# The carry-over product of a windowed-mean pool in a MoE transformer layer: from 128 rows by 64 columns to 32 rows by 16 columns

## The reference, cut to what matters

```python
POOL_WINDOWS = (2, 4, 8, 16)
def multiscale_pool(u, pool_w, pool_scale):        # u: (1, 2048, 512)
    csum0 = jnp.pad(jnp.cumsum(uf, axis=1), ((0, 0), (1, 0), (0, 0)))
    for gi, w in enumerate(POOL_WINDOWS):          # 128 channels for each window
        upper = csum0[:, 1:, lo:hi]
        lower = csum0[:, jnp.maximum(t + 1 - w, 0), lo:hi]
        cnt = jnp.minimum(t + 1, w)
        outs.append((upper - lower) / cnt - uf[:, :, lo:hi])
    ...
h = modulate(rmsnorm(x, norm1_g), shift1, scale1);  proj = h @ w_in      # q, k, v, u
x = x + gate1 * (concatenate([attention(q, k, v), pool(u)]) @ w_out)
x = x + gate2 * moe_ffn(modulate(rmsnorm(x, norm2_g), shift2, scale2))
return rmsnorm(x, final_g)
```

## Time and profile before

| | |
|---|---|
| runs | 2816.91, 2818.95 and 2823.79 us, median 2818.95 |
| profiled execution | 2818.95 us, of which the span is 2817.0 us |
| granted TensorE clock, mean | 0.978 |
| PE busy | 2655.8 us, 94% of the span |
| DVE busy | 1435.9 us, 51% |
| ACT, POOL busy | 839.1 us, 807.4 us |
| chain that ended last | PE 73%, DVE 13%, DMA 8% |

### The profile page before, as it was taken

One profiled execution on the slowest core, in us unless ns is written; L12 is line 12 of the kernel. 1 busy time (PEld: TensorE's weight loads), 2 busy tenths in 40 slices (PEclk: granted clock), 3 DMA queues, 4 the chain that ended last, 5 costly groups with the idle time before them and its releaser, 6 DMA issues.

```text
span 2817.0 us, 46309 instructions
## 1 busy us (share of the span) xinstructions
PE 2655.8 (94%) x13342; PEld 1258.9 (45%) x13343; DVE 1435.9 (51%) x2391; ACT 839.1 (30%) x1304; POOL 807.4 (29%) x460
## 2 busy tenths in 40 slices
PE   4899999998899999999999999999999999999980
PEld 1477887786444333333333333333333333333330
DVE  4578888886433444444444444444444344444345
ACT  3344444443101222222222222222222222222224
POOL 0012222222211333333333233333333333333230
PEclk8999999999999999999999999999999999999995
DMA  8621121214536665888998987989889867869948
GB/s 346 227 76 66 69 75 67 75 67 143 199 111 225 209 212 171 299 286 303 344 337 296 341 299 255 340 291 336 296 297 325 311 180 256 302 212 344 369 115 357
DMA packets 140218, 664.09 MB, mean 236 GB/s; under 512 B 30276, under 2 KB 31173, under 8 KB 87575
## 3 DMA queue, kind: packets, MB, share of 16 engines
q1 hardware_dynamic: 89958, 528.96, 47.4%
q0 software_dynamic: 50224, 134.69, 21.6%
HBM read 569.55 MB, written 127.02 MB: 247 GB/s over the span
## 4 chain that ended last, share of the span: by engine, by line
PE 73%; DVE 13%; DMA 8%; issue 4%; ACT 1%; SPq 1%; DVEq 0%; ACTq 0%; POOLq 0%
PE PB L1497 35%; PE PB L1504 18%; PE PB L1339 5%; DMA arena<-in_w_up_e 5%; PE PB L1250 3%; PE PB L1274 2%; DMA arena<-in_ada_w 1%; PE PB L1510 1%; PE PB L1432 1%; DMA arena<-acc_tab 1%; PE PB L1396 1%; PE PB L1397 1%; PE PB L1401 1%; DVE arena L959 1%; PE PB L1418 1%
## 5 line engine op out<-in xcount | busy, mean ns | idle before, releaser
L1497 PE MATMUL PB<-arena 128*64 x2528 | 1111.5, 592 | 1.1 <-DVE arena L1132 1.1
L1498 PE MATMUL PB<-arena 128*64 128x512 f32 x2528 | 1111.5, 592 | 0.0
L606 POOL DMA_INDIRECT acc_tab<-arena,rec x157 | 480.3, 3059 | 1162.2 <-DVE rec L1168 785.5
L1497 PEld LDWEIGHTS PB<-arena 128*64 128x64 f32 x2528 | 346.5, 137 | 724.6 <-issue 724.6
L1504 PE MATMUL PB<-arena 128*64 x1264 | 606.3, 602 | 2.7 <-ACT arena L751 2.7
L1505 PE MATMUL PB<-arena 128*64 128x512 f32 x1264 | 606.3, 602 | 0.0
L1129 DVE COPY arena<-arena 128x4096 f32 x160 | 367.0, 2294 | 132.1 <-DMA arena<-in_w_up_e 61.1
L1165 DVE SCALAR_TENSOR_TENSOR arena<-PB,RW,arena 128x512 f32<-128x512 f32 x314 | 221.3, 746 | 273.2 <-PE PB L1505 215.9
L1498 PEld LDWEIGHTS PB<-arena 128*64 128x64 f32 x2528 | 346.6, 137 | 0.0
L564 POOL DMA_INDIRECT rec_tab<-recs,posi x128 | 144.2, 1126 | 626.7 <-DVE recs L953 589.9
L1135 DVE TENSOR_TENSOR arena<-arena,PB 128x256 f32<-128x256 f32 x158 | 96.3, 609 | 403.6 <-ACT arena L742 403.6
(11 more groups left out here) (277 smaller groups left out, 2629.8 us busy)
## 6 DMA issues: line engine op xcount, KB each, us to landing
arena<-in_w_gate_e SPq DMA_DIRECT2D x128, 1024.0 KB
arena<-in_w_up_e SPq DMA_DIRECT2D x128, 1024.0 KB, 10.4
arena<-in_w_down_e SPq DMA_DIRECT2D x128, 1024.0 KB, 10.3
arena<-in_ada_w SPq DMA_DIRECT2D x24, 1024.0 KB, 9.3
arena<-in_x SPq DMA_DIRECT2D x32, 512.0 KB, 3.4
acc_tab<-arena SPq DMA_DIRECT2D x32, 512.0 KB, 2.7
arena<-acc_tab SPq DMA_DIRECT2D x6, 2048.0 KB, 22.3
h_tab<-arena SPq DMA_DIRECT2D x16, 512.0 KB, 2.7
```

The source lines that it names most:

```text
L606: g.indirect_dma_start(acc_tab, bass.IndirectOffsetOnAxis(ap=rec[:, n, 1:2], axis=0), ys[n % 2], None, bounds_check=2 * T - 1, oob_is_err= ...
L1497: mm(B[7][0:SUB, :], xTm[:, k, 0:SUB], wa(k), start=(k == 0), stop=(k == KD - 1))
L1498: last = mm(B[7][SUB:P, :], xTm[:, k, SUB:P], WBG[n % 2][:, k], start=(k == 0), stop=(k == KD - 1))
```

## The change

The second product of each channel group uses 32 tokens of `uP` (partitions 96 to 127) in place of 128, and gives 16 output columns in place of 64. The band constant for it gets 16 columns for each group in place of 64, and ACT copies 32 partitions of `uC` to `uP` in place of 128.

```diff
 EDGE = 16
-NEAR = 64
-COLS = dict(ident=P, band0=NPG * EDGE, band=NPG * P, bandp=NPG * NEAR, iota=P,
+COLS = dict(ident=P, band0=NPG * EDGE, band=NPG * P, bandp=NPG * EDGE, iota=P,
             sub=4, half=1, inv=ROT, iotag=NG, tok=NT)
...
-        prev.append(((t - (s - P) < w) / w)[:, 0:NEAR])
+        prev.append(((t - (s - P) < w) / w)[:, 0:EDGE])
...
-                        ch.link(A_(uP, uC, ACT.Copy))
+                        ch.link(A_(uP[96:P, :], uC[96:P, :], ACT.Copy))
...
-                            last = mm(B[7][:, g_ * P:g_ * P + NEAR], uP[:, cs], C("bandp")[:, g_ * NEAR:(g_ + 1) * NEAR], start=False, stop=True)
+                            last = mm(B[7][:, edge], uP[96:P, cs], C("bandp")[96:P, es], start=False, stop=True)
```

## The result

The changed kernel takes 2836.69 us (median of 4 runs, 2831.63 to 2838.24), the kernel before beside it 2819.62 us (2816.91 to 2823.79). The ratio is 1.0055, with a 95% interval of 1.004 to 1.0072: slower by 0.55%, some 16 us. The forecast was slower, 2829.2 us, with a range of 2818 to 2838. The profiled execution took 2837.07 us, its span 2835.0. Two executions in the rounds of the experiments were far off, one of e6_rows64 (5379.73 us) and one of the kernel before (15735.44 us); ratios leave them out.

A forecast was written before the change was run, and what follows sets the result against it. PE was taken to bound the kernel, near balance with DVE. 14 tiles x 1.2 us less 6.5 us spare gave 10.3 us, so 2818.95 + 10.3 = 2829.2 us, range 2818 to 2838.

The forecast's parts named there:

- Columns, load rows, copy, constants: 0 each: Pool's carry product, its weight loads, ACT's copy and the start's constant load: making each smaller was taken to save 0.
- A change of shape, 0.20 in and 0.12 back, 1.2 us a tile: PE's pool: switching between 128-row and 32-row products drains PE, 8 times a tile, 0.32 us a group, 1.2 us a tile.
- Rivals A (under 0.07 us each): Pool: shape changes are cheap and the wait for DVE hides them, 2819 to 2820 us; chance 0.19.
- B (0.28 us each): Pool: shape changes are dear, 0.28 us each, 2.2 us a tile, giving 2843 us; chance of its side 0.08.
- C (a gain): Pool: 32-row loads cost a quarter and nothing drains, at most 1.3 us gained, 2817.6 us; chance 0.04.
- 0.54 us of it hidden in the wait for DVE: Attention-weight transposes behind the pool: PE already waits there for DVE in 12 tiles, hiding 0.54 us, leaving 0.66 us a step.
- the swallowing that was foreseen: DVE's L977 moves by up to 1.0 us, absorbed by 2.13 us of DVE idle time ahead of L999.
- In tile 15 the added time is hidden: Tile 15: PE idles 3.89 us for DVE ahead of L1339, independent of the pool, so its 1.2 us are hidden.
- the likeliest case: Pool's shape changes drain and cost between 0.13 and 0.2 us each, 2827 to 2834 us; chance 0.52.
- a sign for being wrong: The step growing by more than the pool would mean ACT's later L659 reaches PE's output products through its copies.

The follow-up runs named there:

- e6_rows64: Changed kernel with the carry product on the upper 64 rows and 64 partitions copied, in place of 32: 2838.61 us, ratio 1.0045 to the kernel before.
- e1_cols: The whole change except the 32 rows: 16 columns and 32 partitions copied, but the carry product still uses all 128 rows: 2822.51 us, ratio 0.9996.
- the grouped order: Changed kernel with an added zero bf16 product, then four band products and four carry products behind them, 2 shape changes a tile: 2825.48 us, ratio 0.9998.
- The three orders: Changed kernel plus an added zero bf16 product, products ordered for 2, 4 or 8 shape changes a tile: ratios 0.9998, 0.9995 and 1.0031.
- e2_rows: Kernel before with only the carry product put on 32 rows, 64 columns and the full copy kept: 2840.74 us, ratio 1.0054.
- e8_singles: Changed kernel plus an added zero bf16 product, the eight products in the changed kernel's order, 8 shape changes a tile: 2835.74 us, ratio 1.0031.

## Why the prediction was right, and what it missed

*Columns, load rows, copy, constants: 0 each.* Shown for columns, copy and constants by e1_cols (ratio 0.9996, block 1.87 against 1.89 us), and for the rows of the load by its 182 ns and by the grouped order, in which eight products of 32 rows take what eight of 128 do.

*A change of shape, 0.20 in and 0.12 back, 1.2 us a tile.* The block grew by 1.14 us (1.89 to 3.03), and a group takes 0.74 us against the 0.77 that the terms give (0.45 + 0.32). The next pair starts 0.07 us ahead of the recorded end of the last (266.74 against 266.32 + 0.49 = 266.81, and 267.06 against 266.74 + 0.39 = 267.13), the distance that the prediction took from the earlier trace rows. How the 0.29 us of a group part into way in and way back the starts do not settle. The three orders give 0.145 us for each change, e6_rows64 shows it for 64 rows. The rule of the Trainium skill (TensorEngine Tiling (Array Packing), Key Properties), that a change of mode drains the engine, now has rows for 32*128 and 64*128 too. Rivals A (under 0.07 us each), B (0.28 us each) and C (a gain) fall.

*0.54 us of it hidden in the wait for DVE.* Shown: the quiet steps take 36.69 to 36.77 us where most took 36.06 to 36.08, 0.6 to 0.7 us more against the forecast 0.66. The wait of L1417 is gone, and DVE's idle time ahead of L998 (L999 before) fell, since L976 came later, the swallowing that was foreseen. Waits between 150 and 640 us, before and after:

```profile
DVE XT L999 <- ACT arena L700: 27.4, 13, 2.2
...
DVE XT L998 <- ACT arena L699: 7.4, 13, 1.8
```

In tile 15 the added time is hidden, as foreseen: the step from tile 14 to tile 15 takes 34.99 us where it took 34.95. The quiet part of the loss is what is left of the distance when the clock's share (below) is taken off, 20.1 - 10.1 = 10.0 us, forecast as 10.3; by the block it is 14 x 1.14 - 6.5 = 9.5.

*The clock: the step that was left out.* The sum took rows at full clock and let nothing happen to it. Six of the 13 steps between tiles 1 and 14 take 38.31 to 38.46 us and not 36.7, since for 3.4 us the products start 0.43 us apart and not 0.23. Their sum is 230.5 us, six times the quiet mean of 36.73 is 220.4: 10.1 us, 1.7 for each. This doubles the slowdown in the mixing stage, and is why the measured time, 2836.69 us, is near the upper end of the range and outside the 2827 to 2834 us of the likeliest case. That the range still holds it is luck as far as the clock goes: its upper part was meant for changes of up to 0.23 us each, and they cost 0.145. The prediction had a sign for being wrong, a step that grows by more than the pool does; the six long steps grow by 2.3 us where the pool grows by 1.14, but the clock does it, and not ACT's later L659, of which the sign spoke. The same holds for the other counts: e2_rows has a block longer by 1.30 us, 14 x 1.30 - 6.5 = 11.7, and five stretches of 1.6, 19.7 us by this sum against 20.0 measured; e8_singles 14 x 1.26 - 6.5 = 11.1 and two of 1.65, 14.4 against 15.3.

What the engine did before the clock fell is shown as far as this, for 150 to 640 us: in every case it was a pool with eight changes of shape close together, in no case one with 0, 2 or 4 (the 2 and 4 with the added bf16 product in the block), nor one with 8 in two parts. That such a pool is not enough is shown too: the blocks of the tiles between are of the same length and products (266.32 to 269.37 beside 228.01 to 231.06) and keep the clock, and in e8_singles all but two do.

When a pool comes has a part in it. In the five profiles with stretches, 25 in all, the clock falls 2.8 to 3.4 us behind a pool's first load, about when the pool ends. Two falls in a row are 75.1 us apart in all five (once 112.6, in e2_rows), even where the kernel's own rhythm is another: a long and a quiet step together take 75.0 to 75.2 us in the changed kernel, but 75.3 in e2_rows and e8_singles. So the moments of the falls do not follow the kernel's steps exactly, and of equal pools those are hit that lie right for them. What sets the moments was not followed, so the number of stretches could not have been foreseen from these rows.

*Grouped orders.* With two changes the block grows by 0.39 us, less than the spare 0.54, and still the steps take some 0.12 us more than before, and the distance 2.9 us. The cover shrank by 0.28 us a tile (from 6.1 to 2.7 us in 12 tiles) and not by the whole 0.39: what PE waits for there comes 0.11 us later too. Why was not followed.

*Behind the mixing.* The first load of L1417 in tile 15 is 20.8 us later than before, and the first product of the routed experts (L1498 before, L1497 now) is 20.5 us later (871.4 and 891.9 us), so the mixing's loss is passed on. The end of the span is only 18.0 us later. In the routed experts the profile of before has one half-clock stretch of 3.4 us (from 2206.8 us) that the changed kernel's has not. The rest was not followed. It need not be chance: in every version the ratio gives 2 to 7 us less than the distance (in the changed kernel 15.5 against 20.1).

## What to carry to other kernels

A small product on fewer rows of the array was not cheaper for it, but it changes the array's shape: count the changes, put products of one shape together, and price each change by rows of another change of shape in the same kernel, not by the work saved. Where loads set the pace, narrowing the moving side gives nothing. And stalls have a second price: many short ones close together can cost the clock for a while behind them (here 3.4 us at half level, 1.7 us of time, behind six of 13 pools), which the busy share does not show, so look at the granted clock of the stretch that follows.

## What the runs showed of the hardware

A change of the array's shape costs 0.145 us here, way in and way back averaged, for float32 products of 128 and 16 columns, whether to 32 or to 64 rows, and 32-row products in a row cost what full ones do (1.06 and 1.05 us for eight).

The clock fell to half without any gap in PE's busy time (3.40 of 3.40 us in the window ahead of the fall); the stalls are 0.145 us each on average, eight in 3 us. I had taken the clock for safe as long as PE never stood still for long. The Trainium skill (TensorE: Matmul & The Clock Gate, A second HAM failure mode: psum-queue depth-cycling) tells of a kernel in which short idles between groups of products made the clock swing. The rows above show a swing too, behind pools with eight changes of shape; whether it is the same cause no run here shows.
